# Prompt attention of a hybrid decoder step: causal and window masks added by VectorE in PSUM, where TensorE added them as products with the identity

## The chip, the cores and the metric

The kernel runs on one core of a Trainium2 chip. The metric is the device time of one execution in microseconds (us); the median of several runs counts, and lower is better.

## The reference

One layer of a decoder trunk is computed for a prompt of 1024 rows and for 32 sample rows. Each layer has a recurrent head group, an attention head group with three branches (compressed, selected, window), and a feed-forward part. The change touches the prompt's attention alone, in its selected and window branches:

```python
# selected branch; 16 of the 16 blocks are kept, so only the causal mask is left
s = jnp.einsum('bqkgd,bqknld->bqkgnl', qg, kg) * ATTN_SCALE
s = jnp.where(kpos <= q_pos, s, NEG_INF)            # NEG_INF = -1e30
p = jax.nn.softmax(s, axis=-1)
# window branch: the same, with keys of the last 512 positions alone
```

## The kernel before, in words

The whole layer is one program, written engine by engine with semaphores. Its stages run one behind the other: projections and recurrence, keys and values, `prompt_attention` (about 447 to 710 us of the span), then attention of the sample rows, then output projection and feed-forward. Between `prompt_attention` and the next stage stands a barrier of all engines, so a shift of its end shifts what follows.

`prompt_attention` goes through 128 **units** n. There are four **trips** i (one query head of each of the two key heads), in each trip eight query tiles t of 128 rows, for each tile the selected branch (br 1, keys of tiles 0 to t) and the window branch (br 2, keys of the last five tiles at most), and for each branch the two key heads h. Unit 32 i + 4 t + 2 (br - 1) + h has 1 to 8 key tiles of 128 columns. A trip is 32 units; two units with the same tile and branch are a **pair**.

What one unit does, in order, and on which engine:

- TensorE `qk(n)`: scores = queries x keys into one half of two PSUM buffers of two banks each, as two products (`QD` and `QL`, the upper and lower part of the queries), for more than four key tiles in two column halves. Into the same sums it adds the masks: a product of the identity `ident_b` with a 128x128 mask of 0 and -1e30. `diag_b` masks the last key tile, in every unit; `tail_b` masks the first key tile, in window units with t of 4 or more. `qk(n)` waits for the exponential of unit n-2, whose buffer it takes.
- VectorE `top(n)`: waits for the scores, takes the negated row maximum.
- ScalarE `exp(n)`: exponential with row sum, written to SBUF.
- VectorE `weigh(n)`, issued behind `top(n+1)`: one over the row sum.
- GpSimd: scales the probabilities by it and by a gate.
- TensorE `turn(n)`, issued behind `qk(n+3)`: transposes the scaled tiles, the first four into bank 4 (line 1739), the rest into bank 5 (line 1746).
- ScalarE `copy(n)` takes bank 4 to SBUF, VectorE `copy(n)` (line 1919, for units of more than four tiles) takes bank 5. Both banks are single, so `turn` of a unit waits until the copy of the one before is done.
- TensorE `weighted(v)`: the product with the values, for a pair at a time.

Each engine runs its list in order. VectorE's list per step is `top(n)`, `weigh(n-1)`, `copy(n-3)`. In between stand, once a trip each, `stage` (lines 1868 and 1871: the two parts of the next 512 query rows, in the steps n = 3 and 19 of a trip, the latter not in the last trip) and the compressed branch of the next trip (`compress_shift` at step 4, `compress_weigh` at 6, `compress_copy` at 10; not in the last trip). In front of unit 0 GpSimd casts the masks and the identity to the rounded format that these products take (line 1633), and TensorE waits for that.

`s.done(...)` in the diff counts an instruction on VectorE's own semaphore, and `s.fence()` lets VectorE wait until those counted are done.

Of the kernel before, what the change touches and what calls it, by code (L numbers as in the profile page):

```python
# [24 lines left out]
F32R = mybir.dt.float32r  # L25
I32 = mybir.dt.int32
ALU = mybir.AluOpType
# [5 lines left out]
P = 128  # L33
# [171 lines left out]
def sb(nc, stack, name, shape, dt=F32):  # L205
    return stack.enter_context(nc.sbuf_tensor(name, shape, dt))
# [1309 lines left out]
def prompt_attention(k, q_plain, q_rot, qT, qR, kvn, kT, gates, ck_pair, cv_p, attnT, attn_sum, ident, ones, kv_stored, scratch_stored,  # L1516
# [5 lines left out]


    nc, ps, psum, d = k.nc, k.ps, k.psum, k.dram
    (masks_loaded, masks_cast, k_hi_done, k_lo_done, q_hi_done, q_doubled, q_lo_done, gates_picked, v_clear, v_spread, scored, max_ready,
     q_clear, probs_ready, scaled, coef_ready, turned0, turned1, copied0, copied1, out_summed, taken, stepped, cmp_scored, cmp_shifted, cmp_exp, cmp_probs,
     cmp_turned, cmp_copied, queries_spread, squared, rows_summed, sums_taken, pool_stepped) = k.sems(" ".join("s6_" + n for n in (
         "masks_loaded masks_cast k_hi_done k_lo_done q_hi_done q_doubled q_lo_done gates_picked v_clear v_spread scored max_ready "
         "q_clear probs_ready scaled coef_ready turned0 turned1 copied0 copied1 out_summed taken stepped cmp_scored cmp_shifted cmp_exp cmp_probs "
         "cmp_turned cmp_copied queries_spread squared rows_summed sums_taken pool_stepped").split()))  # L1530
    WT = WINDOW // P

    order = [(i, t, br, h) for i in range(KA) for t in range(TILES) for br in (1, 2) for h in range(N_KV)]
# [4 lines left out]
    place = [u % 2 * 1024 + (0 if len(x) <= 4 else 512 - len(x) * P // 2) for u, x in enumerate(tiles_of)]  # L1538
# [13 lines left out]
    KEY_PARTS = [slice(0, HEAD_TILES * P), slice(HEAD_TILES * P, SEQ)]  # L1552
    with ExitStack() as st:

        diag_b, tail_b, ident_b = [sb(nc, st, n, [P, P], F32R) for n in ("diag_r", "tail_r", "ident_r")]
        at = 0

        def take_space(n):
            nonlocal at
            at += n  # L1560
            return space[:, at - n:at]
# [3 lines left out]
        probs = [take_space(SEQ), take_space(SEQ), flat_kT[:, 0:SEQ]]  # L1565
        acc = take_space(SEQ)
        sq = take_space(P)
        diag, tail = probs[0][:, 0:P], probs[0][:, P:2 * P]
        pT = [kvn[:, 0:TILES, 2 * KV_WIDTH:2 * KV_WIDTH + P], flat_kT[:, SEQ:2 * SEQ].rearrange("p (j n) -> p j n", j=TILES)] + [
            kvn[:, 0:TILES, p * P:(p + 1) * P] for p in range(2)]  # L1570
        own = [slice(h * HEAD_DIM, (h + 1) * HEAD_DIM) for h in range(N_KV)]
# [53 lines left out]
        @block.gpsimd  # L1625
        def _(pool):
            for h in range(N_KV):
                pool.memset(QL[h][own[1 - h], :].bitcast(F32), 0.0).then_inc(q_clear, 1)
                pool.wait_ge(q_clear, h + 1)
            pool.memset(vx, 0.0).then_inc(v_clear, 1)  # L1630
            pool.wait_ge(masks_loaded, 48)
            for dst, src in ((ident_b, ident), (diag_b, diag), (tail_b, tail)):
                pool.tensor_copy(dst[:, :], src[:, :]).then_inc(masks_cast, 1)  # L1633
            def spread():
                s = Steps(pool, queries_spread)
                s.then(pool.memset(q_plain[:, :, :], 0.0))
                s.then(pool.memset(q_rot[:, :, :], 0.0))
                for b in range(BT):
                    for h in range(N_KV):
                        part = slice(h * HEAD_DIM, (h + 1) * HEAD_DIM)  # L1640
                        c0 = b * QR + h * DEC_SEQ * GROUP
                        for dst, src in ((q_plain, qT), (q_rot, qR)):
                            for g in range(SG):
                                row = SEQ + (g * BT + b) * DEC_SEQ
                                s.then(pool.tensor_copy(
                                    dst[part, g * BT + b, c0:c0 + DEC_SEQ * GROUP].rearrange("p (s g) -> p s g", g=GROUP),
                                    src[part, :, row:row + DEC_SEQ].rearrange("p g s -> p s g")))
                                yield
            s = Steps(pool, pool_stepped)

            def square(tile):

                i, t = tile // TILES, tile % TILES
                pool.wait_ge(taken, (tile + 1) * N_KV)
                rows = slice(t * P, (t + 1) * P)
                for n, c in enumerate((i // 2, 2 + i // 2)):
                    x = attnT[:, c, rows]
                    if i == 1 and n == 0:
                        s.then(pool.tensor_tensor(acc[:, rows], x, x, ALU.mult))
                        continue  # L1660
                    s.then(pool.tensor_tensor(sq[:, :], x, x, ALU.mult))
                    r = pool.tensor_tensor(acc[:, rows], acc[:, rows], sq[:, :], ALU.add)
                    if i == KA - 1 and n:
                        r.then_inc(squared, 1)
                        pool.wait_ge(squared, t + 1)
                    else:
                        s.then(r)

            steps = spread()
            for n in range(N + 12):  # L1670
                if n < N:
                    w, j = len(tiles_of[n]) * P, slice(n % 4, n % 4 + 1)
                    i, t, br, h = order[n]
                    pool.wait_ge(coef_ready, n + 1)
                    pool.tensor_scalar(probs[n % 3][:, 0:w], probs[n % 3][:, 0:w], coef[:, j],  # L1675
                                       gsel[i % 2][:, t, br, h:h + 1], ALU.mult, ALU.mult).then_inc(scaled, 1)
                    pool.wait_ge(scaled, n + 1)
                if n >= 10 and n % 4 == 2 and (n - 10) // 4 // TILES in (1, KA - 1):
                    square((n - 10) // 4)
                if n < PER:  # L1680
                    next(steps, None)
            for _ in steps:
                pass
            pool.wait_ge(scaled, N)

        @block.tensor
        def _(pe):
# [17 lines left out]
            def qk(n):  # L1705
                i, t, br, h = order[n]
                if n == HEAD_TILES * PER // TILES:
                    pe.wait_ge(k_lo_done, 2 * N_KV)
                if n % PER in (0, PER // 2):
                    need = 2 * N_KV * i + N_KV * (1 + (n % PER) // (PER // 2))  # L1710
                    pe.wait_ge(q_doubled, need)
                    pe.wait_ge(q_lo_done, need)
                if n >= 2:
                    pe.wait_ge(probs_ready, n - 1)
                k0, w, at = tiles_of[n][0] * P, len(tiles_of[n]) * P, place[n]
                tile = slice(t * P, (t + 1) * P)
                masks = {w - P: diag_b}
                if br == 2 and t >= WT:
                    masks[0] = tail_b

                for a, b in ([(0, max(w, 2 * P))] if w <= 512 else [(0, w // 2), (w // 2, w)]):
                    held = [(x, m) for x, m in masks.items() if a <= x < b]
                    keys = slice(k0 + a, k0 + b)
                    pe.matmul(psum[:, at + a:at + b], lhsT=QD[h][:, tile], rhs=KS[h][:, br - 1, keys],  # L1724
                              start=True, stop=False, skip_group_check=True)
                    m = pe.matmul(psum[:, at + a:at + b], lhsT=QL[h][:, tile], rhs=KS[h][:, br - 1, keys],
                                  start=False, stop=not held, skip_group_check=True)
                    for x, mask in held:
                        m = pe.matmul(psum[:, at + x:at + x + P], lhsT=ident_b[:, :], rhs=mask[:, :],  # L1729
                                      start=False, stop=(x, mask) == held[-1], skip_group_check=True)  # L1730
                m.then_inc(scored, 1)

            def turn(n):
# [33 lines left out]
                m.then_inc(out_summed, 1)  # L1767

            compress_scores(0)
            pe.wait_ge(masks_cast, 3)  # L1770
            pe.wait_ge(q_clear, N_KV)
            pe.wait_ge(k_lo_done, N_KV)
            qk(0)
# [16 lines left out]
            for t in range(TILES):  # L1790
                pe.wait_ge(squared, t + 1)
                m = pe.matmul(ps[4][:, 2 * t:2 * t + 2], lhsT=acc[:, t * P:(t + 1) * P], rhs=ones[:, 0:2], start=True, stop=True)
# [66 lines left out]
        def _(dve):  # L1859
            s = Steps(dve, stepped)  # L1860
# [44 lines left out]
            def top(n):  # L1905
                dve.wait_ge(scored, n + 1)
                if n >= 4:
                    dve.wait_ge(probs_ready, n - 3)
                w = len(tiles_of[n]) * P
                dve.tensor_reduce(nmax[:, n % 4:n % 4 + 1], psum[:, place[n]:place[n] + w], AX, ALU.max,  # L1910
                                  negate=True).then_inc(max_ready, 1)

# [1353 lines left out]
```

## Time and profile before

| what | value |
|---|---|
| median of 3 runs | 1706.9 us (1703.04 to 1709.11) |
| the profiled execution | 1706.11 us, of which the span from first to last instruction is 1704.3 us |
| busy in the span: TensorE, weight loads, VectorE, ScalarE, GpSimd | 1609.5, 1483.4, 888.6, 769.0, 441.6 us |
| mean granted TensorE clock | 0.970 of full speed |

Busy times overlap; an engine's idle time costs something only where another engine waits for it. A matmul's duration in the trace holds its latency, and matmuls overlap, so what one matmul costs TensorE is read from start to start.

### The profile page before, as it was taken

How to read it: one execution, taken by the hardware profiler on the slowest of the kernel's cores; microseconds unless marked ns; L12 is line 12 of the kernel's file. 1: busy time of each engine (PE TensorE's matmuls, PEld its weight loads, DVE VectorE, ACT ScalarE, POOL GpSimd, SP SyncE). 2: the span in 40 equal slices, each digit the busy share in tenths (PEclk: the TensorE clock that was granted, in tenths of full speed). 3: DMA queues.
4: the chain of work that ended last, by engine and by line, in shares of the span. 5: the costliest groups of instructions: out<-in, count | busy, mean ns of one | idle time of the engine just before them, and what ended most of it. 6: DMA issues, size and time to landing. Idle time of an engine off the chain costs nothing.

```text
span 1704.3 us, 29622 instructions
## 1 busy us (share of the span) xinstructions
PE 1609.5 (94%) x11171; PEld 1483.4 (87%) x11172; DVE 888.6 (52%) x1481; ACT 769.0 (45%) x1227; POOL 441.6 (26%) x531
## 2 busy tenths in 40 slices
PE   6898999999799999887899999999999999999997
PEld 5687888988687888754899999999999999999997
DVE  3566576675656665455666444434454433444433
ACT  5455245433577677432335554323354322354322
POOL 4222000241354545500464040033050033000032
PEclk9999999999699999888899999999999999999999
DMA  9942555134310001145445445445445445545443
GB/s 338 315 161 58 165 179 147 51 86 137 135 51 1 2 2 57 57 204 225 132 127 147 125 134 136 118 141 159 125 131 164 119 135 150 147 124 169 121 131 91
DMA packets 302013, 221.48 MB, mean 130 GB/s; under 512 B 21061, under 2 KB 289397, under 8 KB 298774
## 3 DMA queue, kind: packets, MB, share of 16 engines
q1 hardware_dynamic: 295412, 179.30, 36.5%
q0 software_dynamic: 5952, 40.76, 6.3%
q8 instruction: 65, 1.06, 0.3%
q14 instruction: 38, 0.31, 0.1%
q10 hardware_dynamic: 546, 0.05, 0.0%
HBM read 212.52 MB, written 11.68 MB: 132 GB/s over the span
## 4 chain that ended last, share of the span: by engine, by line
PE 49%; DVE 1%; ACT 1%; issue 0%; DVEq 0%; ACTq 0%; PEldq 0%
PE banks L626 16%; PE banks L628 16%; PE banks L627 16%; DVE ff_lo L622 1%; ACT ff_hi L618 0%; PE banks L2576 0%; ACT ff_h_hi L618 0%; DVE streams L2900 0%; ACT L618 0%; PE banks L2658 0%; DVE hT L2839 0%; DVE spare_rows L622 0%; ACT merged_hi L618 0%; PE banks L2567 0%; PE banks L2563 0%
## 5 line engine op out<-in xcount | busy, mean ns | idle before, releaser
L622 DVE TENSOR_TENSOR ff_lo<-ff_raw,ff_hi 128x2048 fp32r<-128x2048 f32 (+1 forms) x126 | 265.2, 2105 | 201.8 <-ACT ff_hi L618 201.7
L627 PE MATMUL banks<-low_rows,ff_hi 128*128 128x352 f32 x1120 | 359.1, 321 | 0.0
L626 PE MATMUL banks<-ff_h_hi,ff_hi 128*128 128x352 f32 x1056 | 341.6, 323 | 1.2 <-DVE ff_lo L622 1.2
L628 PE MATMUL banks<-ff_h_hi,ff_lo 128*128 128x352 f32 x1056 | 339.1, 321 | 0.0
L618 ACT ACTIVATE ff_hi<-ff_raw 128x2048 fp32r<-128x2048 f32 (+1 forms) x126 | 215.2, 1708 | 230.5 <-PE banks L628 217.6
L627 PEld LDWEIGHTS banks<-low_rows,ff_hi 128*128 128x128 f32 x1120 | 210.6, 188 | 0.3
L626 PEld LDWEIGHTS banks<-ff_h_hi,ff_hi 128*128 128x128 f32 x1056 | 198.0, 188 | 2.2 <-issue 2.0
L628 PEld LDWEIGHTS banks<-ff_h_hi,ff_lo 128*128 128x128 f32 x1056 | 198.4, 188 | 0.0
L626 PE MATMUL banks<-hid_hi,ff_hi 128*128 128x352 f32 x528 | 171.2, 324 | 4.4 <-DVE hid_lo L622 4.1
L628 PE MATMUL banks<-hid_hi,ff_lo 128*128 128x352 f32 x528 | 169.4, 321 | 0.0
L627 PE MATMUL banks<-hid_lo,ff_hi 128*128 128x352 f32 x528 | 169.2, 320 | 0.0
L1910 DVE TENSOR_REDUCE neg_max<-banks 128x1 f32<-128x640 f32 (+7 forms) x128 | 90.4, 706 | 93.1 <-PE banks L1729 88.5
L618 ACT ACTIVATE hid_hi<-streams 128x352 f32 (+1 forms) x66 | 32.9, 498 | 234.2 <-DVE streams L2900 234.2
L2900 DVE TENSOR_TENSOR streams<-streams,banks 128x352 f32<-128x352 f32 x66 | 34.4, 521 | 139.6 <-PE banks L628 139.5
L626 PEld LDWEIGHTS banks<-hid_hi,ff_hi 128*128 128x128 f32 x528 | 99.0, 188 | 5.4 <-issue 3.8
L626 PE MATMUL banks<-h_hi,s_hi 128*128 128x352 f32 x288 | 101.6, 353 | 1.1 <-DVE h_lo L622 0.7
L627 PEld LDWEIGHTS banks<-hid_lo,ff_hi 128*128 128x128 f32 x528 | 99.4, 188 | 0.0
L628 PEld LDWEIGHTS banks<-hid_hi,ff_lo 128*128 128x128 f32 x528 | 98.9, 187 | 0.0
L628 PE MATMUL banks<-h_hi,s_lo 128*128 128x352 f32 x288 | 93.3, 324 | 0.0
L627 PE MATMUL banks<-h_lo,s_hi 128*128 128x352 f32 x288 | 93.1, 323 | 0.0
L1675 POOL TENSOR_SCALAR hT<-hT,coef,gate_pair 128x640 f32<-128x640 f32 (+7 forms) x86 | 69.3, 806 | 81.3 <-DVE coef L1929 79.2
L1724 PE MATMUL banks<-k_halves,q_doubled 128*128 128x320 f32 (+4 forms) x192 | 79.6, 415 | 3.5 <-POOL tail_r L1633 1.8
(470 smaller groups left out, 3252.5 us busy)
## 6 DMA issues: line engine op xcount, KB each, us to landing
ff_raw<-in_w_gate SPq DMA_DIRECT2D x66, 512.0 KB, 4.0
ff_raw<-in_w_up SPq DMA_DIRECT2D x66, 512.0 KB, 5.3
ff_raw<-in_w_down SPq DMA_DIRECT2D x48, 384.0 KB, 4.1
late_ada<-in_w_ada SPq DMA_DIRECT2D x16, 1024.0 KB, 5.6
ff_raw<-in_w_down SPq DMA_DIRECT2D x48, 320.0 KB, 3.4
ff_raw<-in_w_out SPq DMA_DIRECT2D x24, 512.0 KB, 5.1
early_ada<-in_w_ada SPq DMA_DIRECT2D x4, 2048.0 KB, 27.1
s_raw<-in_w_in SPq DMA_DIRECT2D x48, 128.0 KB, 2.6
```

The lines of the kernel that those rows point to most:

```text
L618: return act.activation(hi, raw, ACT.Copy)
L622: return dve.tensor_tensor(lo, raw, hi.bitcast(F32), ALU.subtract)
L626: pe.matmul(out, lhsT=w_hi, rhs=x_hi, start=first, stop=False)
L627: pe.matmul(out, lhsT=w_hi, rhs=x_lo, start=False, stop=False)
L628: return pe.matmul(out, lhsT=w_lo, rhs=x_hi, start=False, stop=last)
L1675: pool.tensor_scalar(probs[n % 3][:, 0:w], probs[n % 3][:, 0:w], coef[:, j], gsel[i % 2][:, t, br, h:h + 1], ALU.mult, ALU.mult).then_inc( ...
L1724: pe.matmul(psum[:, at + a:at + b], lhsT=QD[h][:, tile], rhs=KS[h][:, br - 1, keys], start=True, stop=False, skip_group_check=True)
L1910: dve.tensor_reduce(nmax[:, n % 4:n % 4 + 1], psum[:, place[n]:place[n] + w], AX, ALU.max, negate=True).then_inc(max_ready, 1)
L2900: dve.tensor_tensor(silu[p], silu[p], ps[2 * (1 - p) + 1][:, 0:GR], ALU.mult).then_inc(mixed, 1)
```

## The change

TensorE no longer adds masks, and the casts on GpSimd fall away with the wait for them. VectorE adds the mask in place to the 128 score columns in PSUM, ahead of the maximum: one addition in every unit, two in window units with t of 4 or more. A fence stands between the additions and the maximum, which reads what they wrote. The masks, kept as fp32, get SBUF tiles of their own, since they are now read to the end; before, they were loaded into space that the probabilities took over.

```diff
-        diag_b, tail_b, ident_b = [sb(nc, st, n, [P, P], F32R) for n in ("diag_r", "tail_r", "ident_r")]
+        diag, tail = [sb(nc, st, n, [P, P]) for n in ("diag", "tail")]
...
-        diag, tail = probs[0][:, 0:P], probs[0][:, P:2 * P]
...
-            pool.wait_ge(masks_loaded, 48)
-            for dst, src in ((ident_b, ident), (diag_b, diag), (tail_b, tail)):
-                pool.tensor_copy(dst[:, :], src[:, :]).then_inc(masks_cast, 1)
...
                 for a, b in ([(0, max(w, 2 * P))] if w <= 512 else [(0, w // 2), (w // 2, w)]):
-                    held = [(x, m) for x, m in masks.items() if a <= x < b]
...
                     m = pe.matmul(psum[:, at + a:at + b], lhsT=QL[h][:, tile], rhs=KS[h][:, br - 1, keys],
-                                  start=False, stop=not held, skip_group_check=True)
-                    for x, mask in held:
-                        m = pe.matmul(psum[:, at + x:at + x + P], lhsT=ident_b[:, :], rhs=mask[:, :],
-                                      start=False, stop=(x, mask) == held[-1], skip_group_check=True)
+                                  start=False, stop=True, skip_group_check=True)
                 m.then_inc(scored, 1)
...
-            pe.wait_ge(masks_cast, 3)
...
                 dve.wait_ge(scored, n + 1)
                 if n >= 4:
                     dve.wait_ge(probs_ready, n - 3)
+                _, t, br, _ = order[n]
                 w = len(tiles_of[n]) * P
+                for at, mask in ((w - P, diag), (0, tail)):
+                    if mask is diag or (br == 2 and t >= WT):
+                        x = psum[:, place[n] + at:place[n] + at + P]
+                        s.done(dve.tensor_tensor(x, x, mask[:, :], ALU.add))
+                s.fence()
                 dve.tensor_reduce(nmax[:, n % 4:n % 4 + 1], psum[:, place[n]:place[n] + w], AX, ALU.max,
                                   negate=True).then_inc(max_ready, 1)
```

On VectorE, first at unit 20 of the first trip, behind the `stage` of step 19. `kT` and `kvn` hold transposed probabilities. Before (lines of the profile):

```order
L1868 TENSOR_SCALAR q_doubled<-streams 64x512 x2
L1871 SCALAR_TENSOR_TENSOR q_lo<-streams,q_doubled 64x512 x2
L1910 TENSOR_REDUCE neg_max<-banks 128x1
L1929 RECIPROCAL coef<-den 128x1
L1919 COPY kT<-banks 128x128
```

And in the changed kernel, whose line numbers differ, from the same place on to unit 22:

```order
L1855 TENSOR_SCALAR q_doubled<-streams 64x512 x2
L1858 SCALAR_TENSOR_TENSOR q_lo<-streams,q_doubled 64x512 x2
L1901 TENSOR_TENSOR banks<-banks,diag 128x128
L1903 TENSOR_REDUCE neg_max<-banks 128x1
L1922 RECIPROCAL coef<-den 128x1
L1912 COPY kT<-banks 128x128
L1901 TENSOR_TENSOR banks<-banks,diag 128x128
L1903 TENSOR_REDUCE neg_max<-banks 128x1
L1922 RECIPROCAL coef<-den 128x1
L1912 COPY kvn<-banks 128x128
L1901 TENSOR_TENSOR banks<-banks,diag 128x128
L1901 TENSOR_TENSOR banks<-banks,tail 128x128
```

The additions stand ahead of each maximum, and so ahead of the copy out of bank 5 that follows it in the list.

On TensorE, the two window units of tile 4 in the first trip (18 and 19) and the start of unit 20. Before:

```order
L1724 MATMUL banks<-k_halves,q_doubled 128x320
L1726 MATMUL banks<-k_halves,q_lo 128x320
L1729 MATMUL banks<-tail_r,ident_r 128x128
L1724 MATMUL banks<-k_halves,q_doubled 128x320
L1726 MATMUL banks<-k_halves,q_lo 128x320
L1729 MATMUL banks<-diag_r,ident_r 128x128
L1739 MATMUL banks<-ident_m,hT 128x128 x4
```

In the changed kernel the same unit reads:

```order
L1715 MATMUL banks<-k_halves,q_doubled 128x320
L1717 MATMUL banks<-k_halves,q_lo 128x320
L1715 MATMUL banks<-k_halves,q_doubled 128x320
L1717 MATMUL banks<-k_halves,q_lo 128x320
L1727 MATMUL banks<-ident_m,hT 128x128 x4
```

Two products fewer stand in the unit, and the scores count as done with the last `q_lo` product. The order of everything else is as before.

## Rows read from the trace of the kernel before

**Rows 1.** By stretch: length, busy PE, PEld, DVE, ACT, POOL (count), clock, DMA share, rate.

```profile
447.00:710.00 263.00, 246.89 (x2228) 213.01 (x2228) 156.08 (x399) 185.01 (x466) 135.14 (x215) 0.95 0.07 27
...
529.50:532.90 3.40, 3.40 (x15) 2.71 (x15) 2.19 (x9) 2.10 (x7) 1.26 (x3) 0.51 0.00 0
```

**Rows 2.** Groups by line, 445 to 709 us: busy, mean ns | idle ahead, releasers.

```profile
L1729 PE MATMUL banks<-diag_r,ident_r 128*128 128x128 f32 x128 | 29.8, 233 | 0.0
...
L1910 DVE TENSOR_REDUCE neg_max<-banks 128x1 f32<-128x640 f32 (+7 forms) x128 | 90.4, 706 | 93.1 <-PE banks L1729 88.5 <-ACT hT L1812 3.2
...
L1883 DVE TENSOR_TENSOR cmp_probs<-banks,hT 128x256 f32<-128x256 f32 x4 | 1.6, 410 | 0.0
```

**Rows 3.** Groups by line and shape on VectorE, 447 to 710 us.

```profile
L1919 DVE COPY kvn<-banks 128x128 f32<-128x128 f32 x36 | 10.0, 277 | 4.0 <-PE banks L1746 4.0
...
L1910 DVE TENSOR_REDUCE neg_max<-banks 128x1 f32<-128x128 f32 x16 | 4.6, 286 | 10.2 <-PE banks L1729 10.1
```

**Rows 4.** TensorE in order of time, unit 14: start, duration, engine, line, operation.

```profile
475.32 0.39 PE L1726 MATMUL banks<-k_halves,q_lo 128*128 128x512 f32 x1
475.55 0.22 PE L1729 MATMUL banks<-diag_r,ident_r 128*128 128x128 f32 x1
475.61 0.49 PE L1739 MATMUL banks<-ident_m,kT 128*128 128x128 f32 x3
```

**Rows 5.** VectorE in order of time, two fenced instructions of the compressed branch.

```profile
460.77 0.41 DVE L1883 TENSOR_TENSOR cmp_probs<-banks,hT 128x256 f32<-128x256 f32 x1
461.21 0.42 DVE L1884 TENSOR_REDUCE cmp_stat<-cmp_probs 128x16 f32<-128x256 f32 x1
```

**Rows 6.** VectorE in order of time, first trip, maxima of units 2 and 8.

```profile
456.81 0.28 DVE L1910 TENSOR_REDUCE neg_max<-banks 128x1 f32<-128x128 f32 x1
...
466.66 0.56 DVE L1910 TENSOR_REDUCE neg_max<-banks 128x1 f32<-128x384 f32 x1 [1.01 <-PE banks L1729]
```

**Rows 7.** ScalarE and TensorE in order of time: end of unit 5's exponential, start of qk(7).

```profile
463.35 0.19 ACT L1812 ACTIVATION_READ_ACCUMULATOR kT<-banks,neg_max 128x1 f32 x1
...
463.60 0.58 PE L1724 MATMUL banks<-k_halves,q_doubled 128*128 128x256 f32 x1
```

**Rows 8.** VectorE and TensorE in order of time, first trip, units 19 to 21.

```profile
484.35 0.82 DVE L1910 TENSOR_REDUCE neg_max<-banks 128x1 f32<-128x640 f32 x1 [0.30 <-PE banks L1729]
...
489.32 0.27 DVE L1919 COPY kT<-banks 128x128 f32<-128x128 f32 x1
...
489.64 0.33 PE L1746 MATMUL banks<-ident_m,hT 128*128 128x128 f32 x1 [0.72 <-DVE kT L1919]
```

**Rows 9.** In order of time, second trip, units 35 to 39: TensorE, VectorE, ScalarE.

```profile
528.42 0.30 PE L1739 MATMUL banks<-ident_m,kT 128*128 128x128 f32 x1 [1.43 <-ACT kvn L1822]
...
528.77 0.16 DVE L1929 RECIPROCAL coef<-den 128x1 f32<-128x1 f32 x1 [0.67 <-ACT hT L1812]
...
530.56 0.42 DVE L1910 TENSOR_REDUCE neg_max<-banks 128x1 f32<-128x256 f32 x1
...
531.01 0.47 ACT L1812 ACTIVATE hT<-banks,neg_max 128x256 f32<-128x256 f32 x1 [1.00 <-DVE neg_max L1910]
```

**Rows 10.** TensorE in order of time, fourth trip, start of qk(102).

```profile
654.91 0.39 PE L1724 MATMUL banks<-k_halves,q_doubled 128*128 128x256 f32 x1 [0.28 <-ACT hT L1812]
```

**Rows 11.** VectorE and TensorE in order of time, first trip, units 21 to 26.

```profile
496.83 1.09 DVE L1910 TENSOR_REDUCE neg_max<-banks 128x1 f32<-128x896 f32 x1 [1.87 <-PE banks L1729]
497.83 0.15 DVE L1929 RECIPROCAL coef<-den 128x1 f32<-128x1 f32 x1
497.90 0.41 DVE L1919 COPY kT<-banks 128x256 f32<-128x256 f32 x1
...
498.60 0.27 PE L1746 MATMUL banks<-ident_m,hT 128*128 128x128 f32 x1
...
502.36 0.27 DVE L1919 COPY kvn<-banks 128x128 f32<-128x128 f32 x1
...
503.19 0.49 PE L1746 MATMUL banks<-ident_m,hT 128*128 128x128 f32 x3
```

More of the change, by code:

```diff
@@ L1524, in prompt_attention @@
     nc, ps, psum, d = k.nc, k.ps, k.psum, k.dram
-    (masks_loaded, masks_cast, k_hi_done, k_lo_done, q_hi_done, q_doubled, q_lo_done, gates_picked, v_clear, v_spread, scored, max_ready,
+    (masks_loaded, k_hi_done, k_lo_done, q_hi_done, q_doubled, q_lo_done, gates_picked, v_clear, v_spread, scored, max_ready,
      q_clear, probs_ready, scaled, coef_ready, turned0, turned1, copied0, copied1, out_summed, taken, stepped, cmp_scored, cmp_shifted, cmp_exp, cmp_probs,
      cmp_turned, cmp_copied, queries_spread, squared, rows_summed, sums_taken, pool_stepped) = k.sems(" ".join("s6_" + n for n in (
-         "masks_loaded masks_cast k_hi_done k_lo_done q_hi_done q_doubled q_lo_done gates_picked v_clear v_spread scored max_ready "
+         "masks_loaded k_hi_done k_lo_done q_hi_done q_doubled q_lo_done gates_picked v_clear v_spread scored max_ready "
          "q_clear probs_ready scaled coef_ready turned0 turned1 copied0 copied1 out_summed taken stepped cmp_scored cmp_shifted cmp_exp cmp_probs "
@@ L1716, in qk @@
                 tile = slice(t * P, (t + 1) * P)
-                masks = {w - P: diag_b}
-                if br == 2 and t >= WT:
-                    masks[0] = tail_b
                 for a, b in ([(0, max(w, 2 * P))] if w <= 512 else [(0, w // 2), (w // 2, w)]):
-                    held = [(x, m) for x, m in masks.items() if a <= x < b]
                     keys = slice(k0 + a, k0 + b)
```

## The prediction

> **What bounds the kernel now.** I first asked which engine the attention stage waits for. The busy times by stretch give TensorE 246.9 of 263 us, ScalarE 185, VectorE 156 [rows 1]. The grouped view says who waits: ahead of its 128 maxima VectorE sat idle for 93.1 us, 88.5 of them until a mask product of TensorE had ended [rows 2]. So over most of the stage TensorE sets the pace and VectorE stands ready. That is an average, so I then read the stage in order of time, and looked for the places where TensorE waits for something that hangs on a maximum. There are four kinds, and they decide:
>
> - The start, first trip. From unit 2's maximum on VectorE has work at hand, and unit 8's, some 10 us later, is the first that waits again (1.01 us) for scores [rows 6]. `qk(7)` starts 0.06 us behind the end of unit 5's exponential (463.54 to 463.60) [rows 7]: TensorE follows VectorE here.
> - Tile 1 of the second and third trip, where the compressed branch of the next trip is put in. ScalarE waits 1.00 us for unit 39's maximum, TensorE 1.43 us for a copy that stands behind the compressed exponential [rows 9].
> - Tile 1 of the fourth trip: `qk(102)` waits 0.28 us for an exponential [rows 10].
> - Unit 18's transpose into bank 5 in the first three trips. It waits 0.72 us for VectorE's copy of unit 17, which stands behind both halves of `stage` [rows 8].
>
> **What the change costs and saves, per instruction.** On TensorE 160 products fall away: 128 with the diagonal mask, and 4 trips x 4 tiles x 2 heads = 32 with the tail mask. The mean of 233 ns [rows 2] is latency; what one costs is its start to the next start, 475.55 to 475.61, so 0.06 us [rows 4]. All 160 are 9.6 us, and that is the most the change can bring. Scores are also done 0.06 us earlier per mask.
>
> On VectorE 160 additions of 128 columns are new. The trace has none that writes PSUM in place. A copy of 128 columns out of PSUM takes 277 ns, a maximum over 128 columns of PSUM 286 ns [rows 3], and an addition with one input in PSUM takes 410 ns for 256 columns [rows 2]. I take 0.28. Below, 0.27 is the bound; above, the 0.41 of the 256-column addition, in case a write to PSUM costs more than one to SBUF. The fence: behind the fenced addition that ends at 461.17 the next starts at 461.21, so 0.04 us [rows 5]. An instruction without a wait starts 0.08 to 0.09 us before the end of the one ahead (497.83 against 497.92) [rows 11], so a second mask adds about 0.20. One mask: 0.32, less the 0.06 of the earlier scores = **+0.26 us** until the maximum. Two: 0.52 - 0.12 = **+0.40 us**. VectorE's time rises by 96 x 0.32 + 32 x 0.52 = 47 us, from 156 to about 200 of 263.
>
> Half of such a small addition is not columns: from 128 to 256 columns the time rises by 0.13 us only [rows 2, 3]. The Trainium skill says the same of VectorE (VectorE: DVE Perf Modes, section on the TRN2 errata): a fixed latency per instruction, to be spread over tiles of 512 elements or more, and 120 + 128 cycles at 0.96 GHz for a source in PSUM, an estimate of 0.26 us. By that the additions would be 160 x 0.02 = 3 us cheaper in VectorE's time, and my sum below some 0.5 us lower; it speaks against the change all the same.
>
> The casts on GpSimd that `qk(0)` waited for fall away. I count nothing: unit 0's maximum stands behind the compressed branch on VectorE anyway.
>
> **Place by place**, as a shift of TensorE against before:
>
> 1. First trip, start. Six additions (units 2 to 7) lengthen VectorE's run by 1.9 us. What TensorE waits for is unit 5's exponential, and four additions stand ahead of that: 4 x 0.32 = 1.3 at `qk(7)`. From there TensorE does its own work, four to five masks less, and part of what ran at the lower clock comes later, at full clock: I take **+0.9**.
> 2. Tile 1, second and third trip. Unit 36's addition delays the compressed branch, unit 39's its own maximum; those of 37 and 38 fill the 0.67 us that VectorE waits for an exponential [rows 9]. 0.26 + 0.32 = +0.6 each, **+1.2**.
> 3. Tiles 1 to 3, fourth trip. Here each exponential is waited for; two to three additions come through in a row before later slack takes them: 0.26 x 3 = **+0.8**.
> 4. `stage`, three trips. Ahead of unit 17's copy stand the additions of units 18, 19 (two masks each) and 20: 0.52 + 0.52 + 0.32 = 1.36. Unit 18's scores come 0.12 earlier, and VectorE had 0.30 idle ahead of unit 19's maximum [rows 8]. 1.36 - 0.42 = +0.94 each, **+2.8**. TensorE's idle time there grows from 0.72 to about 1.9 us, since it also arrives some 0.24 earlier.
> 5. The rest, tiles 4 to 7 and tile 0, where TensorE is the bound. Here it should gain 0.06 per mask, but a short detour opens: in unit 24's step the copy of unit 21 stands behind unit 24's maximum, ends at 498.31, and unit 22's transpose into bank 5 starts at 498.60 [rows 11], 0.29 us of slack less the 0.05 us that a release takes. The copy comes +0.26 later, so TensorE can't start earlier than now: the gain of units 24 and 25 is gone. In the window pairs the same slack is 0.56 (502.63 to 503.19) [rows 11], the copy comes 0.40 later, and of 0.24 saved some 0.1 stays. Over tiles 4 to 7 that leaves 0.2 to 0.4 per trip instead of 24 x 0.06 = 1.4, and tile 0 leaves 0.2: together **-2.1**.
>
> Sum: 0.9 + 1.2 + 0.8 + 2.8 - 2.1 = **+3.6 us** at an unchanged clock.
>
> 6. TensorE's clock. It fell from 2.4 to 1.2 GHz for 3.4 us (0.51 granted) [rows 1] right behind the idle 1.43 us of tile 1 [rows 9]; behind the 0.72 us at `stage` it stayed up. The new 1.9 us there is longer than both. Where TensorE is the bound, a fall costs up to 3.4 x 0.49 = 1.7 us; I take 1.5. The place can fall well or badly, three times: I count two falls, **+3.0**.
>
> Together +6.6. The profiled execution took 1706.1 us (span 1704.3), 0.8 below the median of the runs. 1706.1 + 6.6 = 1712.7; against the median 1713.5. I forecast **1713 us**.
>
> **Rivals.**
>
> - *The clock holds.* The idle time at `stage` grows, but no lower clock follows, as it did not behind 0.72 us [rows 8]. Then only the +3.6 stay: 1710, within 0.3% of before (that is 1701.8 to 1712.0, about what a measurement of this kernel can tell from no change). For it: most of the stage runs at full clock now (0.95) [rows 1]. Against: 1.43 us of idle time was enough once. Chance 0.42, with cases in which the detours cost a little less.
> - *TensorE is relieved* (the other side). VectorE's copy and maximum are early enough everywhere but at `stage` and the start, and TensorE keeps its 0.06 per mask: from the 9.6 us come off about 3 at places 1 to 4, so 1706.1 - 6 = 1700. It decides if the detour of place 5 has more slack than the 0.29 us read. For it: 88.5 us in which VectorE waited for TensorE [rows 2]. Against: the slack is needed in the same step, not on average. Chance 0.08. The Trainium skill (Perfetto Trace Analysis, section Identifying the Most-Contended Engine) has a rule to the same end: kernels generally gain where the engine with the highest occupancy is relieved, TensorE being judged by its weight loads. Here that engine is TensorE, 213 of 263 us [rows 1]; by this rule the time falls.
> - *The addition in place is dear.* At 0.41 instead of 0.28 every addition on a path costs 0.13 more: at places 1 to 4 about 4 + 4 + 3 + 15 of them, +3.4, and in place 5 six detours a trip with one or two additions, some +1.2 a trip. That gives 1713 + 8 = 1721. Nothing speaks for it but the missing row.
>
> **Numbers.** The forecast (about 1711 to 1716) has 0.38, the dear addition or a third and fourth fall of the clock 0.12, the clock holding 0.42, the relief 0.08. So faster by over 0.3%: 0.08, within: 0.42, slower: 0.50. For 8 in 10 the range runs from 1704, where some relief is left, to 1720: that takes in the bounds of the addition but for its last us.
>
> **What would show it.** In the new profile: 160 additions of 0.27 to 0.30 us on VectorE; its idle time ahead of maxima falls from 93 to some 50 us; the L1746 transposes wait longer for VectorE, above all at `stage` (1.9 us instead of 0.72); stretches of half clock behind them, two more than before; the stage ends 3 to 7 us later. Wrong would be: additions far from 0.28 us, no longer wait at `stage`, or tiles 4 to 7 shorter by over 1 us a trip.

## The result and the profile after

The changed kernel is slower: 1717.3 us median of six runs (1712.12 to 1719.12), beside 1708.19 us for the kernel before in the same series; the ratio is 1.0054, 95% interval 1.0037 to 1.0072. A second series gave 1719.51 and 1.0065 (1.0041 to 1.0088). The forecast was 1713, a loss of 6.6 us or 0.39%; the first interval takes that in, the second just misses it, and the sign was right. The median itself lies 4.3 us above the forecast, above the 1711 to 1716 that the prediction meant by it and within its wider range of 1704 to 1720.

The profiled execution took 1712.12 us, the shortest of the six, its span 1709.9. First the stage, by windows (columns as in rows 1): the whole stage, then the four stretches of lower clock in tiles 0 to 3 of the later trips.

```profile
447.00:717.00 270.00, 247.45 (x2086) 197.93 (x2088) 193.29 (x558) 187.64 (x466) 134.66 (x214) 0.92 0.07 26
529.10:535.90 6.80, 6.68 (x30) 4.85 (x30) 4.14 (x14) 3.97 (x14) 2.32 (x4) 0.50 0.01 4
590.55:593.95 3.40, 3.37 (x23) 2.77 (x20) 1.52 (x5) 0.56 (x2) 0.86 (x2) 0.50 0.00 0
597.40:604.20 6.80, 6.67 (x29) 4.82 (x29) 3.88 (x14) 3.75 (x13) 3.49 (x7) 0.50 0.00 0
662.25:665.65 3.40, 3.40 (x14) 2.42 (x14) 2.22 (x8) 2.26 (x7) 1.13 (x3) 0.50 0.86 334
```

Against [rows 1], TensorE's busy time is about the same, VectorE's is up by 37 us, and the granted clock of the stage is down from 0.95 to 0.92. The one stretch of 3.4 us at about 530 us has become 6.8 us long.

The groups by line and shape on VectorE, 447 to 717 us (L1901 the additions):

```profile
L1901 DVE TENSOR_TENSOR banks<-banks,diag 128x128 f32<-128x128 f32 x128 | 37.7, 294 | 64.3 <-PE banks L1717 63.6
...
L1901 DVE TENSOR_TENSOR banks<-banks,tail 128x128 f32<-128x128 f32 x32 | 9.3, 290 | 0.0
```

160 additions take 47.0 us, 0.29 each. The wait for scores now stands ahead of the addition; it was 88.5 us [rows 2] and is still 63.6. VectorE has spare time on average, and that doesn't help. The waits of the same stretch (engine and line, what for: us in all, times, longest) say who pays:

```profile
DVE banks L1901 <- PE banks L1717: 63.6, 56, 2.3
...
ACT hT L1799 <- DVE neg_max L1903: 17.3, 34, 1.8
...
ACT kT L1799 <- DVE neg_max L1903: 11.5, 17, 4.0
...
PEld banks L1734 <- DVE kT L1912: 6.5, 11, 1.6
```

The same three in the kernel before, 447 to 710 us:

```profile
ACT kT L1812 <- DVE neg_max L1910: 5.9, 4, 3.8
...
ACT hT L1812 <- DVE neg_max L1910: 5.4, 9, 1.3
...
PEld banks L1746 <- DVE kT L1919: 3.0, 3, 1.1
```

ScalarE waits 28.8 us for maxima, 51 times, where it waited 11.3 us, 13 times. L1734 is the transpose into bank 5 (L1746 before), whose weight loads wait 6.5 us for VectorE's copy, L1912, where they waited 3.0. Three of these waits stand behind `stage`, once in each of the first three trips, as before. The eight others are new: in every trip unit 22's transpose waits some 0.25 us and unit 26's 0.29, in tiles 6 and 7. The place where this is longest is unit 18's transpose behind `stage`. In the first trip, in order of time: VectorE from unit 20 on, then TensorE.

```profile
488.19 0.30 DVE L1901 TENSOR_TENSOR banks<-banks,diag 128x128 f32<-128x128 f32 x1
...
489.47 0.27 DVE L1912 COPY kT<-banks 128x128 f32<-128x128 f32 x1
```

```profile
488.01 0.63 PE L1727 MATMUL banks<-ident_m,hT 128*128 128x128 f32 x4 [0.50 <-ACT kT L1809]
489.79 0.33 PE L1734 MATMUL banks<-ident_m,hT 128*128 128x128 f32 x1 [1.15 <-DVE kT L1912]
```

The addition, the maximum and the reciprocal still stand between `stage` and the copy; TensorE's 0.72 us of [rows 8] have become 0.50 and 1.15.

To see where the time went, place by place, I took from each trace the start of every unit's first score product, less that of unit 0, and subtracted the same of before. All kernels of this study, one profiled execution each, us:

```
kernel                    start  stage  t 6-7  other tiles 0-3, trips 2/3/4    end | half
before                    +0.00  +0.00  +0.00  +0.00   +0.00  +0.00  +0.00   +0.00 | 27.1
changed                   +0.89  +2.60  +0.16  -1.77   +1.30  +2.46  +1.26   +6.88 | 41.3
changed, again            +0.89  +3.92  +0.12  -1.23   +1.46  +2.45  +0.43   +8.04 | 41.9
no masks                  -0.03  -0.11  -2.49  -2.00   -1.09  -0.33  -0.37   -6.42 | 23.6
both                      +0.90  +3.97  +2.04  +0.33   +2.13  +1.54  +0.70  +11.61 | 37.1
TensorE tiles 0-1         +0.00  +3.94  +0.11  -1.05   +1.31  -0.28  +0.23   +4.26 | 34.6
TensorE tiles 4-7         +0.77  +0.00  -0.01  +0.81   -0.43  +0.82  +1.18   +3.16 | 33.7
changed, stage 17         +0.88  -3.23  +0.10  +2.00   +0.94  -0.21  +0.42   +0.90 | 30.3
before, stage 17          +0.01  -3.10  -0.02  +1.67   -0.60  +1.26  +0.01   -0.78 | 28.1
every second unit         +0.00  -3.12  -0.52  +1.38   +1.61  +0.04  +0.00   -0.61 | 30.9
... and copy first        +0.89  -3.29  -0.78  +0.67   +1.70  +1.53  +0.44   +1.16 | 34.7
before, both moves        +0.00  -3.11  -0.03  +1.24   +0.29  +0.50  -0.02   -1.13 | 27.1
all three moves           -0.00  -3.29  -0.81  +0.74   -0.76  +1.11  +0.23   -2.79 | 27.1
second unit, copy first   +0.01  -3.12  -0.48  +1.17   +0.28  +1.75  -0.00   -0.39 | 30.4
```

Columns: *start*, units 0 to 8; *stage*, units 20 to 22 of three trips; *t 6-7*, tiles 6 and 7 of all trips (24 to 32; 120 to 127 in the last); tiles 0 to 3 of trips 2, 3 and 4; *other*, the rest; *end*, at unit 127; *half*, us of the stage at the lower clock. ("... and copy first" belongs to the changed kernel with `stage` at step 17.) `start`, `stage` and `t 6-7` repeat between kernels to a few hundredths where the clock is the same; the tiles 0 to 3 don't. Taking unit 0 as zero hides little: it starts 5.43 us behind VectorE's first `stage` instruction in the kernels with the casts on GpSimd, and 5.32 us behind it in those without.

### The profile page after: what moved, and what is told of

Same layout as the page of the kernel before. It is cut to its first block, busy times and chain, and to the rows that moved or that the text cites. A ratio compares the mean times of both kernels' runs of the same rounds, so it can differ in the third digit from the quotient of the medians.

```text
span 1709.9 us, 29459 instructions
## 1 busy us (share of the span) xinstructions
PE 1610.8 (94%) x11011; PEld 1469.5 (86%) x11012; DVE 926.9 (54%) x1641; ACT 771.7 (45%) x1227; POOL 440.7 (26%) x528
## 4 chain that ended last, share of the span: by engine, by line
PE 49%; DVE 1%; ACT 1%; issue 0%; DVEq 0%; ACTq 0%; PEldq 0%
PE banks L626 16%; PE banks L628 16%; PE banks L627 16%; DVE ff_lo L622 1%; ACT ff_hi L618 0%; DVE hT L2832 0%; PE banks L2569 0%; ACT ff_h_hi L618 0%; DVE streams L2893 0%; ACT L618 0%; PE banks L2651 0%; DVE spare_rows L622 0%; ACT merged_hi L618 0%; PE banks L2560 0%; PE banks L2556 0%
## 5 line engine op out<-in xcount | busy, mean ns | idle before, releaser
L618 ACT ACTIVATE ff_hi<-ff_raw 128x2048 fp32r<-128x2048 f32 (+1 forms) x126 | 215.2, 1708 | 228.8 <-PE banks L628 216.9
L1671 POOL TENSOR_SCALAR hT<-hT,coef,gate_pair 128x640 f32<-128x640 f32 (+7 forms) x86 | 69.1, 804 | 89.8 <-DVE coef L1922 88.5
```

The costliest lines, as they stand in the source:

```text
L618: return act.activation(hi, raw, ACT.Copy)
```

## The experiments

Each kernel was timed in five rounds, those of one series beside the same runs of the kernel before (1707.97 us in the first series of four, 1707.48 in the second, 1708.56 in the third). Ratios are to that, with their 95% interval.

**TensorE's relief alone** ("no masks"). The changed kernel without its additions:

```diff
-                for at, mask in ((w - P, diag), (0, tail)):
...
-                        s.done(dve.tensor_tensor(x, x, mask[:, :], ALU.add))
-                s.fence()
```

> The changed kernel without VectorE's additions, so that no masks are added anywhere (causal and window masks of the prompt's attention are left out). Theory (the loss comes from maxima that come later): only TensorE's relief is left, so tiles 4 to 7 gain about 1.4 us a trip, tiles 0 to 3 some 0.3, the wait at `stage` falls back to about 1 us: 5 to 7 us below before, some 14 below the changed kernel. Rival (the additions are not to blame, but what else moved: SBUF places, the casts gone from GpSimd): it stays near the changed kernel, 5 us or more above before.

Measured: 1702.01 us, 0.9968 (0.9952 to 0.9984). TensorE's busy time in the stage falls to 238.82 us, against 246.89 in [rows 1]:

```profile
447.00:710.00 263.00, 238.82 (x2104) 195.58 (x2104) 157.12 (x401) 185.07 (x468) 136.91 (x218) 0.95 0.07 27
```

So the 160 products were worth 6 us of the 9.6 at most. In tiles 6 and 7 it is 0.62 us a trip for 12 masks (2.49 / 4), 0.05 each. The change doesn't fail because TensorE's work is hidden; it gives all of it back, and more. What else moved with the change (SBUF places, the casts) moved in this kernel too, and isn't to blame.

**The additions alone** ("both"). The kernel before, which keeps TensorE's masks, with VectorE's additions on top:

```diff
                 w = len(tiles_of[n]) * P
+                for at, mask in ((w - P, diag_b), (0, tail_b)):
...
+                        s.done(dve.tensor_tensor(x, x, mask[:, :].bitcast(F32), ALU.add))
+                s.fence()
```

> The kernel before, with its products on TensorE, and VectorE's additions on top (each mask is added twice, which leaves the softmax as it is). Theory: TensorE's relief was worth little in the changed kernel, since the copies behind the maxima hold it, so this is only 1 to 4 us slower than the changed kernel. Rival (the relief was worth most of its 9.6 us and the additions cost nearly 19): about 9 us slower than the changed kernel.

Measured: 1716.66 us, 1.006 (1.0042 to 1.0078): about as slow as the changed kernel, though TensorE does 160 products more. By the medians the rival's 9 us are out; the 1 to 4 us of the theory lie within the two intervals. Its trace ends the stage 4.7 us later than that of the changed kernel (11.61 against 6.88), which the medians don't show. Tiles 6 and 7 alone are cleaner: the additions cost 0.51 us a trip (2.04 / 4), the relief is worth 0.62, the two together leave 0.04. There, relief and additions nearly cancel.

**Where the additions hurt: tiles 0 and 1 or tiles 4 to 7.** Two kernels share the masks out by tile: in the first TensorE keeps tiles 0 and 1, in the second tiles 4 to 7. VectorE skips those. The first one's edit against the changed kernel, beside the products and casts that come back (the second has `t >= 4` where this has `t <= 1`):

```diff
+                masks = {w - P: diag_b} if t <= 1 else {}
...
+                if not (t <= 1):
+                    for at, mask in ((w - P, diag_b), (0, tail_b)):
```

> TensorE adds the masks in tiles 0 and 1 (32 of 160), VectorE in tiles 2 to 7. Theory: the shifts at the start and at tile 1 vanish (some 3 us), and with them the added stretches at the lower clock that stand behind them (some 4 us); what stays is the wait at `stage`: 6 to 8 us below the changed kernel, within 4 us of before. Rival (each addition costs about the same wherever it stands): 32/160 of the loss of 9 us, so 2 us below the changed kernel.

Measured: 1712.97 us, 1.0022 (1.0006 to 1.0038): 4.3 us below the changed kernel's median, 5.5 by the ratios, between the 6 to 8 of the theory and the 2 of the rival. The loss at the start is gone (0.00 instead of 0.89). At tile 1 it still fell to the lower clock, and at `stage` of the second trip it fell for 3.4 us more.

> VectorE adds the masks in tiles 0 to 3 (64 of 160), TensorE in tiles 4 to 7: the other half of the run with tiles 0 and 1 on TensorE. Theory: start +0.9, tile 1 +0.6 twice, fourth trip +0.8, and added stretches at the lower clock behind them; nothing at `stage` or after it: 3 to 7 us above before. Rival (the loss is one of `stage` alone): within 1 us of before.

Measured: 1713.12 us, 1.004 (1.0024 to 1.0056), 5.6 us above before and within the 3 to 7 expected. The loss at `stage` is gone (0.00), that at the start remains (0.77). So both places were what the prediction took them for; neither alone brings the kernel back.

**The stall at `stage`.** `stage` two steps earlier, in the changed kernel and in the kernel before:

```diff
-    FIRST_HALF_AT = PER // 2 + 3
+    FIRST_HALF_AT = PER // 2 + 1
```

> The changed kernel with the first half of `stage` two steps earlier (step 17 instead of 19 of a trip), where no copy out of bank 5 waits behind it. Theory: TensorE's wait at unit 18's transpose goes (about 1.3 to 1.7 us, three times), and VectorE's 2 us of idle time ahead of unit 18's maximum takes most of `stage`: 3 to 5 us below the changed kernel. Rival (VectorE has no room left for it in tile 4): no change, the wait moves to unit 18's exponential.

Measured: 1710.79 us, 1.0022 (1.0008 to 1.0036), 6.5 us below the changed kernel's median and 5.5 by the ratios, where 3 to 5 were expected. In its trace the weight loads of L1734 wait 2.1 us for the copy, where they waited 6.5, and never longer than 0.3:

```profile
PEld banks L1734 <- DVE kT L1912: 2.1, 8, 0.3
```

> The kernel before with the first half of `stage` at step 17 of a trip instead of 19. Theory: TensorE's wait of 0.72 us at unit 18's transpose goes, three times, and little comes in its place: 1 to 2.5 us below before. Rival: the earlier `stage` delays the maximum of unit 18 and with it qk(20) by as much: no change.

Measured: 1706.22 us, 0.999 (0.9981 to 1.0), within the 1 to 2.5 us below before that were expected, though the interval just reaches no change at all. The columns *stage* and *other* must be read together here, since the halves now stand among units 16 to 19: -1.4 for the kernel before (-3.10 + 1.67), and, against the changed kernel's +0.83, -1.23 for the changed one, thus 2.1 us, or some 3.2 without the longer lower clock in the first trip (30.7 us instead of 27.3). The earlier place is worth more where the additions stand. The tiles 0 to 3 give another 3.9 us (1.15 against 5.02 in the three columns), with 6.8 us at the lower clock there instead of 20.4; together that is the 6.0 us by which the stage ends earlier (0.90 against 6.88). So about 2 to 3 us belong to the earlier `stage`; whether it also spared the lower clock in tiles 0 to 3 isn't shown, since that falls elsewhere from one execution to the next.

**The changed kernel again.**

> The changed kernel as it is, for a second profile and more rounds. Theory: the shift of TensorE by place (start +0.9, `stage` +0.7 to +0.9 in each of the first three trips, tiles 6 and 7 near zero) comes again within 0.2 us, while the stretches at the lower clock fall in other places. If the shifts by place move as much as the clock does, the place by place account has no ground. Time: 1713 to 1719.

Measured: 1719.51 us, 1.0065 (1.0041 to 1.0088), just above the 1713 to 1719 expected. Places repeat (start 0.89, `stage` 0.87 and 0.86 in the first two trips, tiles 6 and 7 0.12 in all), but the lower clock falls elsewhere: not in the fourth trip, yet behind `stage` in the third, which takes 2.18 for that. TensorE at that place, then the window:

```profile
629.74 0.33 PE L1734 MATMUL banks<-ident_m,hT 128*128 128x128 f32 x1 [1.16 <-DVE kT L1912]
```

```profile
629.90:633.30 3.40, 3.40 (x25) 2.85 (x25) 1.22 (x3) 2.46 (x7) 1.63 (x2) 0.51 0.02 5
```

At 1.16 us of idle time the clock fell here; at 1.15 us in the first trip of the other execution it didn't.

**Additions only in the second unit of a pair**, tiles 4 to 7, with `stage` at step 17.

```diff
-                masks = {w - P: diag_b}
+                masks = {w - P: diag_b} if t < 4 or h == 0 else {}
...
+                if not (t < 4 or h == 0):
+                    for at, mask in ((w - P, diag_b), (0, tail_b)):
```

> VectorE adds the masks only in the second unit of each pair of tiles 4 to 7 (48 of 160), TensorE all others, and the first half of `stage` stands at step 17. Theory: the copy that holds TensorE stands behind the maximum of the first unit of a pair, so these additions are hidden, TensorE keeps 12 x 0.06 = 0.7 us a trip, and the wait at `stage` is gone: 3 to 5 us below before. Rival (an addition delays TensorE in either unit): no better than the kernel before with `stage` at step 17.

Measured: 1705.98 us, 0.9995 (0.9983 to 1.0007): as the kernel before with `stage` at step 17, not the 3 to 5 us below before that were expected. Tiles 6 and 7 gain 0.13 us a trip (0.52 / 4) for 6 masks, where 0.31 could be had at 0.05 each.

**The copy out of bank 5 as the path.** VectorE's list per step turned round, in four kernels:

```diff
-                if n - 1 < N:
-                    weigh(n - 1)
                 if 0 <= n - 3 < N:
                     copy(n - 3)
+                if n - 1 < N:
+                    weigh(n - 1)
```

First in the changed kernel with `stage` at step 17:

> The changed kernel with `stage` at step 17, and VectorE's list per step turned round: the copy out of bank 5, then the reciprocal, where the reciprocal stood first. The copy then starts about 0.07 us earlier (its start less the reciprocal's, 498.15 to 498.22 in the trace of the changed kernel). Theory (the copy out of bank 5 is the path by which the additions eat TensorE's relief in tiles 5 to 7): some ten copies a trip are waited for, so 0.4 to 0.7 us a trip come back, 1.5 to 2.5 us in all against the kernel with `stage` at step 17 alone (1710.8), and tiles 6 and 7 of a trip, which were as long as before (+0.03 to +0.06 us, where the kernel without masks has -0.62), become shorter by 0.2 to 0.4 us. Rival (the path runs over maximum and exponential to the next scores): nothing changes there, and the time stays within 0.7 us.

Measured: 1708.9 us, 1.0007 (0.9994 to 1.002), against 1.0022 without the move: 2.6 us by the ratios. The intervals of the two overlap, but the places are clear: tiles 6 and 7 are 0.20 us shorter a trip than before (0.78 / 4) where they were 0.03 longer. VectorE's copy of unit 21 and the weight load of unit 22's transpose, which waits for it; first in the changed kernel with `stage` at step 17, then with the move on top:

```profile
499.67 0.40 DVE L1912 COPY kT<-banks 128x256 f32<-128x256 f32 x1
...
500.12 0.14 PEld L1734 LDWEIGHTS banks<-ident_m,hT 128*128 128x128 f32 x1 [0.25 <-DVE kT L1912]
```

```profile
497.12 0.41 DVE L1912 COPY kT<-banks 128x256 f32<-128x256 f32 x1
...
497.58 0.14 PEld L1734 LDWEIGHTS banks<-ident_m,hT 128*128 128x128 f32 x1 [0.19 <-DVE kT L1912]
```

In both, the weight load starts 0.05 us behind the copy's end (500.07 and 497.53) and the transpose 0.06 us behind it; in the kernel before, the transpose started 0.29 us behind it [rows 11]. With the copy 0.07 us earlier the wait is 0.06 us shorter, 0.19 instead of 0.25. Either trace has eight such waits, unit 22's and unit 26's in each trip (2.1 and 1.6 us in all), so two a trip and not the ten that were expected. The copy is the path, or the longest part of it: the two waits became 0.13 us shorter a trip, tiles 6 and 7 0.22. Then the same in the kernel before with `stage` at step 17:

> The kernel before with `stage` at step 17 and the copy out of bank 5 ahead of the reciprocal: no additions. By the prediction the copy has 0.29 us of slack here, so an earlier copy is worth nothing: the time is that of the kernel before with `stage` at step 17 (1706.2) within 0.7 us, and tiles 6 and 7 keep their length within 0.05 us a trip. If they become shorter by 0.2 us a trip or more, the slack was not there, and the copy is on TensorE's path in the kernel before too.

Measured: 1706.47 us, 0.9988 (0.9976 to 1.0001); tiles 6 and 7 as before (-0.03 in four trips). Without additions the slack is there, and no wait of a weight load of this transpose for the copy is in the trace (none of 0.15 us or more).

> All three mends together: TensorE keeps the masks of tiles 0 and 1, VectorE adds those of tiles 2 to 7, `stage` at step 17, the copy out of bank 5 ahead of the reciprocal. If the places add up (start 0, `stage` -0.9 each, tiles 6 and 7 -0.2 to -0.4 a trip, tile 1 as with TensorE's masks), the end of the attention stage comes 2 to 3.5 us earlier than in the kernel before and the time is 1704 to 1706, better than both kernels. Rival (tiles 2 to 5 have detours of their own): no better than the kernel before with `stage` at step 17, 1706 to 1708.

Measured: 1703.31 us (1699.82 to 1708.38), **0.9974 (0.996 to 0.9989)**: the only version with additions that is clearly below the kernel before, by 4.4 us (0.0026 x 1708.56). The end of the stage comes 2.79 us earlier, within the 2 to 3.5 expected. Its profiled execution spent 27.1 us at the lower clock, as long as before. Not all of this is due to the additions: the kernel before with the same two moves and no additions took 1706.47 us (0.9988) and ended the stage 1.13 us earlier, also with 27.1 us at the lower clock. Beside that one the additions in tiles 2 to 7 bring 1.7 us in the traces and 2.4 by the ratios, and the two intervals overlap.

> VectorE adds the masks only in the second unit of each pair of tiles 4 to 7 (48 masks; TensorE keeps the other 112), `stage` at step 17, the copy out of bank 5 ahead of the reciprocal. Without the earlier copy such a kernel took 1705.98, and tiles 6 and 7 had got 0.12 us shorter a trip, where 6 masks less there could give 0.36. Theory (the copy is the detour): 0.1 to 0.25 us more a trip, 0.5 to 1 us in all, 1705 to 1705.5. Rival: no change.

Measured: 1706.89 us, 0.9991 (0.9978 to 1.0004), tiles 6 and 7 -0.12 us a trip, as without the move. The rival holds: with TensorE's mask in the first unit of the pair the copy isn't what these units wait for. Neither this trace nor that without the move has a weight load of the transpose that waits for it (0.15 us or more). So the copy was freed as planned; what keeps the rest of the relief (0.12 of 0.31 us a trip came) is open.

## Why the prediction was right, and where it was not

- **The sum at unchanged clock (+3.6).** Start: +0.9 forecast, +0.89 measured. `stage`: +2.8 forecast, +2.60 measured (0.87 in each trip). Place 5: -2.1 forecast; -1.77 + 0.16 = -1.6 measured, and tile 0 of two later trips, which stands in the other columns, adds about -0.15 each. In tiles 4 to 7, units 20 and 21 aside, 0.26 to 0.40 us a trip were left, where 0.2 to 0.4 was forecast; with no additions it was 1.02 to 1.09. Tiles 6 and 7, where the slack was read, are as long as before: the detour over the copy eats the whole relief, 0.25 + 0.29 us of waits a trip against 0.62, and the moved copy shows it. The casts, counted as nothing, were worth 0.1 us at unit 0.
- **Tile 1 (+1.2 and +0.8, tile 0's -0.2 a trip still to come off).** Mis-sized, a little high. The fourth trip at full clock is +0.43, in three traces, where 0.8 - 0.2 = 0.6 was forecast. In the second trip, where the clock stayed up, the kernel with additions in tiles 0 to 3 took -0.43, those with TensorE's masks in tiles 0 and 1 -0.60 and -0.76: 0.2 to 0.3 us for the additions, not 0.4.
- **The clock (+3.0): the step that failed in its place.** I put two falls behind the idle time at `stage`. In the first profiled execution no stretch followed there; instead tiles 0 to 3 of the later trips hold 20.4 us at the lower clock where before held 6.8, four stretches of 3.4 us more. One of them costs 0.8 to 1.3 us: 0.83 in the fourth trip (1.26 against 0.43), 0.9 and 1.3 in the second trip of the kernels without additions there (-0.60, +0.29, +1.61 with none, one and two). I take 1.0, so 4 us in place of 3.0: the size of the term was near, at another place. That is luck: what I took for the cause, the longer idle time at `stage`, brought none of these four, and the count was four and not two. The median of 1717.3 lies where the prediction had put a third and fourth fall, with the dear addition (chance 0.12 for both). Of the measured 6.9 that leaves 2.9 for the terms at unchanged clock, where 3.6 was forecast. The falls behind `stage` do exist: once in the changed kernel's second profile, and once each in "both" and "TensorE tiles 0-1", in 3 of 12 such places of these four traces.
- **Prices.** Addition 0.294 and 0.290 us for 0.28. The estimate of 0.26 from the Trainium skill (VectorE: DVE Perf Modes, section on the TRN2 errata) was 10 to 12% low; the same section's formula for fp32 additions of two tensors, (N + 151) cycles at 0.96 GHz, which it states for N of 512 and 2048, gives 0.291 for N = 128, an estimate that the trace bears out (0.290 to 0.294). The dear addition (0.41) is out. Start to start, a mask took 0.33 us and the second of a pair of masks 0.20 (medians), for 0.32 and 0.20; that makes 48 us in VectorE's list, for 47. Its busy time rose by 37 us only, to 193 and not to about 200: the 47.0 us of the additions' own durations overlap with their neighbours', and the gap of a fence isn't busy.
- **Too optimistic:** VectorE's idle time ahead of scores fell to 64 us, not 50. The idle time at `stage` came as 0.50 and 1.15 us, not as one wait of 1.9.
- **The rivals.** *TensorE is relieved* named 6 us, and the relief alone is worth 6; the numbers meet by chance, since the rival's 6 was 9.6 less some 3 for the additions, and the measured 6 is without any. It lost since the relief is taken back in the same steps. The rule of the Trainium skill (Perfetto Trace Analysis, section Identifying the Most-Contended Engine) names the engine to relieve. That engine was relieved by 15 us of weight loads (213.0 to 197.9), and the time rose by 0.5%; with the relief alone (195.58) it fell by 0.3%, as the rule says. What turned it is the price of the moved work in VectorE's list. *The clock holds* did not come about: both profiles of the changed kernel have 14 to 15 us more at the lower clock than before.

Still open: the medians differ by 9 and 12 us, the stage by 6.9 and 8.0 in the traces. The first interval, 6.3 to 12.3 us (0.0037 and 0.0072 of 1708), takes both 6.9 and 9 in; whether the executions that weren't profiled lost more to the clock was not seen. Outside the stage executions differ too: unit 0 starts 444.2 to 451.5 us into the span over these fourteen traces. The second profile of the changed kernel is 11.8 us above that of before; 8.0 of it is the stage, and 3.7 is a later unit 0. Why the lower clock falls more often in tiles 0 to 3 of the changed kernel also stays open.

## What to carry to other kernels

Work moved from the busiest engine to an idle one still lands in that engine's queue: look for what stands behind it there, here a copy that frees a PSUM bank, and compare its slack (0.29 us) with the added time (0.32 us), step by step and not on average. What helped here was to leave the additions out in tiles 0 and 1, where the start waits for the maxima, and to put the freeing copy ahead of what can wait: with 128 of the 160 additions, `stage` earlier and the copy first, the time went from +0.54% to -0.26%, where the two moves without any addition gave -0.12%. Choosing the units by the copy alone (the second of a pair) didn't pay. Time the relief without its price and the price without its relief; they need not cancel everywhere.

## What the runs showed of the hardware

The same idle time of TensorE brought a lower clock in one execution and none in another. The Trainium skill (TensorE: Matmul & The Clock Gate, section What's actually happening) says that the gate's watch isn't started by the kernel, so that the moment of a change varies; these executions agree, and no run here tests it. In the kernel with TensorE's masks in tiles 4 to 7, TensorE waited 1.71 us at tile 1 of the second trip, as in the changed kernel, and kept 2.4 GHz. The changed kernel's row, behind which the clock fell to 1.2 GHz, then that kernel's rows and window:

```profile
528.53 0.30 PE L1727 MATMUL banks<-ident_m,kT 128*128 128x128 f32 x1 [1.71 <-ACT kvn L1809]
```

```profile
532.92 0.30 PE L1739 MATMUL banks<-ident_m,kT 128*128 128x128 f32 x1 [1.71 <-ACT kvn L1822]
...
536.46 0.44 PE L1724 MATMUL banks<-k_halves,q_doubled 128*128 128x384 f32 x1 [1.24 <-ACT hT L1812]
```

```profile
533.00:536.40 3.40, 2.15 (x13) 1.28 (x13) 3.19 (x12) 1.91 (x9) 1.24 (x3) 1.00 0.00 0
```

At full clock it was done sooner and sat idle for 1.24 us more: the score product behind that idle time started 3.54 us after the first row, and the same product of the changed kernel, at half the clock, 3.55 us after (532.08). So up to there the lower clock cost nothing; by the columns a stretch in these tiles cost about 1 us and not the 1.7 that its length would. Over the traces, kernels with additions in tiles 0 and 1 spent 6.8 to 20.4 us of the later trips' tiles 0 to 3 at the lower clock (six traces, mean 13.6), those with TensorE's masks there 6.8 to 10.2 (seven, mean 8.3); the one without any masks spent 3.4. That points to the additions as the cause of more falls; with one trace of most kernels and the ranges overlapping it isn't settled.
